# Gated heads: the two widest levels block by block without a mask, the six others masked and summed in the diagonal 32x32 blocks

## The chip, the cores and the metric

The kernel runs on one core of a Trainium2 chip. The metric is device time in microseconds (us) of one execution, as the median of several runs. The engines named below are PE (matrix multiplies), DVE (vector), ACT (activations and copies), POOL and SP (the queue that issues the weight DMAs). Each engine works through its own instructions in order and waits on semaphores for the others.

## The reference, cut to what matters

The whole program is a four-layer model on 256 tokens. The change touches only the gated linear attention in two of the layers: "GLA" with 4 heads (value width 256) and "HGRN" with 8 heads (value width 128).

```
def chunked_gated_linear_attention(q, k, v, log_g):
    '''S_t = diag(g_t) S_{t-1} + k_t^T v_t ; o_t = q_t S_t, evaluated chunkwise.'''
    bc = jnp.cumsum(blocks(log_g), axis=2)
    ...
        inter = jnp.einsum('bihk,bhkv->bihv', qi * jnp.exp(bi), state)
        decay = jnp.exp(jnp.where(causal, bi[:, :, None] - bi[:, None, :], -jnp.inf))
        scores = jnp.einsum('bihk,bjhk,bijhk->bhij', qi, ki, decay)
        intra = jnp.einsum('bhij,bjhv->bihv', scores, vi)
```

## The kernel before

**The stream of weights.** Everything is organised around chunks of 512x512 weights in float32. SP loads chunk i into the ring `WF`. ACT writes its bf16 high half, `hi(i)` (L974), DVE the remainder as a bf16 low half, `lo(i)` (L1464), which waits for `hi(i)`. PE multiplies each chunk in three products per tile, 48 matmuls of 256 columns in `gemm` (L513). ACT and DVE work three chunks ahead (`LA` = 3), on rings of five.

**Flows beside it.** All other work is written as Python generators. Every engine has one queue of such flows (`Side`) and takes a step of the first flow at fixed places: with `rate=3`, ACT and DVE take three steps after each hi or lo, and PE takes one step in the middle of a chunk and two at its end. A flow has the same number of steps on each engine, so step s of a head lies at the same chunk everywhere, but an engine reaches it only after all that is written in front of it. This order is fixed when the program is built.

**A head of the gated attention** (`gla_heads`, once for each engine) works on two halves m of 128 tokens, with the scores split by eight levels: level 0 is the diagonal, level l the pairs that lie in the same block of 2^l tokens but in different halves of it. It takes 8 steps, numbered 0 to 7:

- PE: step 0 products of half 0 (eight 128x128 float32 matmuls into banks 0 and 1 of `PB`, and the cross product into bank 2), step 1 the norm sum of the head in front (it needs bank 2, which the cross copy frees), step 2 products of half 1, step 6 scores times values, `weighted`, which reads `RED`.
- DVE: step 1 and step 3, for half 0 and half 1, multiply the 128x1024 products by the mask `lmask` into `MS` (L1903) and sum over the levels into `RED` (L1907); at step 3 also the scaling of the head in front (L1924, it needs `s_rms`); step 4 `weigh(h+1)`, 16 multiplies (L1893); step 5 `decay(h+2)`, 15 subtractions (L1881 to L1883).
- ACT: step 0 copy and square of the output of the head in front (L1086, L1089), step 1 the cross copy (L1274), step 2 the norm of the head in front by Ln and Exp (L1095, L1097), each with a table load, step 7 the exponentials of h+2 (L1266), which need `decay(h+2)`.

In HGRN, the flow begins late and the heads lie beside the last gate, the `glu` and the `cd_out0` products. Heads are counted from 0 in each layer.

Of the kernel before, what the change touches and what calls it, by code (L numbers as in the profile page):

```python
# [195 lines left out]
def two_block_model(nc, A, out):  # L196
    ctx = ExitStack()
    with ctx:
# [3 lines left out]
        def sem(name):  # L202
# [50 lines left out]
        s_tab, s_tabv, s_cp, s_ang5, s_rot5 = (  # L253
            sem(n) for n in ("s_tab", "s_tabv", "s_cp", "s_ang5", "s_rot5"))

        s_decp, s_gabs, s_lg, s_ones, s_scan, s_dec, s_dexp, s_wgh, s_prod, s_ms, s_cross, s_xc, s_red = (
            sem(n) for n in ("s_decp", "s_gabs", "s_lg", "s_ones", "s_scan", "s_dec", "s_dexp", "s_wgh", "s_prod",
                             "s_ms", "s_cross", "s_xc", "s_red"))
        s_dil, s_gy, s_gh, s_gl = (sem(n) for n in ("s_dil", "s_gy", "s_gh", "s_gl"))

        s_bu, s_br, s_mg, s_sscan, s_xs, s_yb, s_ty, s_uh, s_ul = (
# [173 lines left out]
        def gpsimd_program():  # L435
# [28 lines left out]
            nc.gpsimd.wait_ge(s_xl, x_ready(4)[-1][1])  # L464
            nc.gpsimd.wait_ge(d_csst, 16 * 16)
            nc.gpsimd.wait_ge(d_cwst, 16 * 8)
            t = own.mark(nc.gpsimd.memset(GLA["MS"], 1.0))
            nc.gpsimd.wait_ge(g_own, t)
            nc.gpsimd.memset(GLA["MS"].rearrange("p (m w) -> p m w", w=128)[:, :, 0:1], 0.0).then_inc(s_ones, 1)
# [18 lines left out]
            for n in range(16):  # L488
                if n % 2 == 0 and n // 2 + 2 < 8:
                    nc.gpsimd.wait_ge(s_bu, n + 2)  # L490
                    b_load(n // 2 + 2)
                if n < 14:
                    nc.gpsimd.wait_ge(s_xs, n + 1)
                    rotation_load(n + 2)
                if n % 2 and n < 15:
                    nc.gpsimd.wait_ge(s_yb, n + 1)
                    nc.gpsimd.dma_start(CW, CWD[n // 2 + 1]).then_inc(d_cwld, 16)

        def tensor_program():
# [261 lines left out]
            def gla_heads(P):  # L763
# [3 lines left out]
                def head(h):  # L767
                    n = base + h
                    kk, qq, e = k[:, h, :], q[:, h, :], E[h % 2]
                    for m in range(2):  # L770
                        c = slice(128 * m, 128 * m + 128)
                        nc.tensor.wait_ge(s_wgh, n + 1)
                        free(0)
                        for l in range(8):
                            lhs, rhs = (kk[:, c], qq[:, c]) if l == 0 else (e[:, l - 1, c], e[:, l - 1, c])
                            last = mm(PB[:, l // 4, 128 * (l % 4):128 * (l % 4) + 128], lhs, rhs, l % 4 == 0, True)
                        last.then_inc(s_prod, 1)
                        bank_free[0] = (s_ms, 2 * n + m + 1)
                        if m == 0:
                            free(2)  # L780
                            mm(PB[:, 2, 0:128], e[:, 7, 0:128], e[:, 7, 128:256], True, True).then_inc(s_cross, 1)
                            bank_free[2] = (s_xc, n + 1)
                        yield
                        yield
                    yield
                    yield
                    nc.tensor.wait_ge(s_xc, n + 1)
                    nc.tensor.wait_ge(s_red, 2 * n + 2)
                    weighted(P["v"], 128 * nv * h, nv, RED)
                    yield  # L790
                    yield
# [171 lines left out]
        def scalar_program():  # L963
# [33 lines left out]
            def idle(n):  # L997
                for _ in range(n):
                    yield
# [256 lines left out]
            def gla_heads(P):  # L1256
                H, nv, base, E, RED = P["H"], P["nv"], P["base"], P["E"], P["RED"]

                def exponentials(h):
# [5 lines left out]
                    nc.scalar.wait_ge(s_dec, n + 1)  # L1265
                    act(e, e, ACT.Exp).then_inc(s_dexp, 1)  # L1266

                def head(h):
                    n = base + h
                    yield  # L1270
                    nc.scalar.wait_ge(s_cross, n + 1)
                    if h:
                        nc.scalar.wait_ge(s_pv, P["pv"] + h)
                    act(RED[:, 128:256], PB[:, 2, 0:128], ACT.Copy).then_inc(s_xc, 1)  # L1274
                    yield from idle(6)
                    if h + 2 < H:
                        exponentials(h + 2)
                    yield
# [118 lines left out]
            def hgrn():  # L1397
                while "idd" not in flags:
                    yield
                nc.scalar.wait_ge(s_scan, 2)  # L1400
                nc.scalar.wait_ge(s_ul, 2)
                yield from gla_heads(HGRN)

            nc.scalar.wait_ge(s_gam, 1)
# [49 lines left out]
        def vector_program():  # L1454
# [411 lines left out]


            def gla_heads(P):
                H, nv, base, E, RED, MS = P["H"], P["nv"], P["base"], P["E"], P["RED"], P["MS"]

                def decay(h):
                    n, bb, e = base + h, P["b"][:, h, :], E[h % 2]
# [23 lines left out]
                def head(h):  # L1896
                    n = base + h
                    for m in range(2):
                        yield
                        nc.vector.wait_ge(s_prod, 2 * n + m + 1)  # L1900
                        if 2 * n + m:
                            nc.vector.wait_ge(s_red, 2 * n + m)
                        tt(MS, PB[:, 0:2, :].rearrange("p a b -> p (a b)"), cn("lmask"), ALU.mult).then_inc(s_ms, 1)  # L1903
                        nc.vector.wait_ge(s_ms, 2 * n + m + 1)
                        if h:
                            nc.vector.wait_ge(s_pv, P["pv"] + h)
                        nc.vector.tensor_reduce(RED[:, 256 * m:256 * m + 128], MS.rearrange("p (l t) -> p t l", l=8),  # L1907
                                                AX.X, ALU.add).then_inc(s_red, 1)
                        yield
                    if h + 1 < H:  # L1910
                        weigh(h + 1)
# [336 lines left out]
```

## Time and profile before

| | |
|---|---|
| median of 3 runs | 3239.39 us (3235.76 to 3240.88) |
| the profiled execution: its time, its span | 3238.17 us, 3236.9 us |
| PE busy, share of the span | 3062.1 us, 95% |
| DVE busy | 2151.3 us, 66% |
| ACT busy | 1527.1 us, 47% |
| mean granted clock of PE | 0.978 of full speed |

Matmuls overlap, so PE's busy share says that its queue was seldom empty, not that it was at its peak. What the change can be worth is read from the stretches in which PE waits, and from who is waited for there.

### The profile page before, as it was taken

What the parts mean: (1) busy time and instruction counts of PE and PEld (TensorE: products, weight loads), DVE (VectorE), ACT (ScalarE), POOL (GpSimd) and SP (SyncE); (2) the same over time, 40 slices, a digit from 0 to 9 for tenths busy, and PEclk for the clock granted to TensorE, in tenths of its full rate; (3) what the DMA queues carried; (4) which work ended last, traced back from release to release, by engine and by line L of the source; (5) the groups of instructions that cost most, each with busy time, mean ns of one, the idle gap of its engine ahead of it and who ended that gap; (6) DMA issues with size and microseconds to landing.
All of it is one profiled execution on the core that took longest, in us unless ns stands there. A gap on an engine that the chain in (4) does not pass through costs nothing. (4 is left out here: it accounts for less than half of the span.)

```text
span 3236.9 us, 57237 instructions
## 1 busy us (share of the span) xinstructions
PE 3062.1 (95%) x25845; PEld 2603.8 (80%) x25870; DVE 2151.3 (66%) x2204; ACT 1527.1 (47%) x1406; POOL 64.5 (2%) x112
## 2 busy tenths in 40 slices
PE   8999999999999999999999999998999899888786
PEld 7888788888888787588888888886687777657685
DVE  5555866666555666468687776545765557998785
ACT  4343655444433544745455554335544534324543
POOL 0000000000000000001200000000000001000000
PEclk9999999999999999999999999999999999899898
DMA  8665455565565454455766566553445445554331
GB/s 285 209 208 183 148 204 196 208 209 201 204 206 200 154 180 159 157 169 170 267 228 218 206 224 244 196 182 120 163 149 196 151 163 203 172 189 156 113 118 66
DMA packets 295476, 596.75 MB, mean 184 GB/s; under 512 B 11824, under 2 KB 16048, under 8 KB 295104
## 3 DMA queue, kind: packets, MB, share of 16 engines
q1 hardware_dynamic: 287616, 564.22, 51.1%
q0 software_dynamic: 7616, 28.87, 2.4%
q8 instruction: 203, 3.33, 0.4%
q14 instruction: 41, 0.34, 0.0%
HBM read 577.32 MB, written 15.73 MB: 183 GB/s over the span
## 5 line engine op out<-in xcount | busy, mean ns | idle before, releaser
L1464 DVE TENSOR_TENSOR WL<-WF,WH 128x2048 bf16<-128x2048 f32 x533 | 1206.8, 2285 | 692.6 <-ACT WH L974 692.4
L506 PE MATMUL PSG<-XH,WH 128*128 128x256 bf16 x5648 | 1552.4, 275 | 49.8 <-DVE XL L1569 24.1
L506 PE MATMUL PSG<-XL,WH 128*128 128x256 bf16 x5648 | 1551.7, 275 | 0.0
L506 PE MATMUL PSG<-XH,WL 128*128 128x256 bf16 x5648 | 1551.4, 275 | 0.0
L974 ACT ACTIVATE WH<-WF 128x2048 bf16<-128x2048 f32 x533 | 1000.2, 1899 | 617.2 <-PE PSG L506 381.5
L506 PE MATMUL PSG<-SCR,WH 128*128 128x256 bf16 x4480 | 738.5, 273 | 0.0
L506 PEld LDWEIGHTS PSG<-XH,WH 128*128 128x128 bf16 x5648 | 557.1, 99 | 132.0 <-issue 62.4
L506 PEld LDWEIGHTS PSG<-XL,WH 128*128 128x128 bf16 x5648 | 556.9, 99 | 70.7 <-issue 0.8
L506 PEld LDWEIGHTS PSG<-XH,WL 128*128 128x128 bf16 x5648 | 556.8, 99 | 68.8
L506 PE MATMUL PSG<-SCR,WL 128*128 128x256 bf16 x2240 | 611.2, 273 | 0.0
L506 PEld LDWEIGHTS PSG<-SCR,WH 128*128 128x128 bf16 x4480 | 439.2, 98 | 55.8 <-issue 0.3
L506 PEld LDWEIGHTS PSG<-SCR,WL 128*128 128x128 bf16 x2240 | 219.5, 98 | 25.8
L506 PE MATMUL PB<-SCR 128*128 128x128 f32 (+3 forms) x928 | 165.3, 346 | 56.0 <-DVE SCR L2084 31.0
L506 PEld LDWEIGHTS PB<-SCR 128*128 128x128 f32 (+2 forms) x928 | 137.2, 206 | 78.9 <-DVE SCR L2084 35.6
L1688 DVE SCALAR_TENSOR_TENSOR SCR<-PSG,PR,SCR 128x254 f32<-128x254 f32 (+1 forms) x352 | 143.9, 474 | 52.5 <-ACT SCR L1147 51.4
L1147 ACT ACTIVATE SCR<-PSG,PR 128x256 f32<-128x256 f32 x176 | 85.0, 562 | 100.2 <-PE PSG L506 100.2
L506 PE MATMUL PSG<-WL,XH 128*128 128x512 bf16 x314 | 119.5, 381 | 1.0 <-issue 0.5
L995 ACT ACTIVATE SCR<-PSG 128x1024 f32<-128x1024 f32 x34 | 34.7, 1021 | 181.6 <-PE PSG L506 181.6
L506 PE MATMUL PSG<-WH,XL 128*128 128x512 bf16 x314 | 119.3, 380 | 0.3
L506 PE MATMUL PSG<-WH,XH 128*128 128x512 bf16 x307 | 116.9, 381 | 0.3
L1158 ACT ACTIVATE SCR<-SCR 128x1024 bf16<-128x1024 f32 x22 | 23.3, 1057 | 96.4 <-DVE SCR L1697 96.4
L506 PEld LDWEIGHTS PSG<-WH,XL 128*128 128x128 bf16 x320 | 31.4, 98 | 38.1 <-issue 0.6
(240 smaller groups left out, 1554.2 us busy)
## 6 DMA issues: line engine op xcount, KB each, us to landing
WF<-ffn_w_up SPq DMA_DIRECT2D x176, 1024.0 KB, 5.8
WF<-ffn_w_down SPq DMA_DIRECT2D x88, 1024.0 KB, 5.1
WF<-ab_w_in SPq DMA_DIRECT2D x56, 1024.0 KB, 5.2
WF<-a_w_in SPq DMA_DIRECT2D x48, 1024.0 KB, 5.9
WF<-cd_w_in SPq DMA_DIRECT2D x48, 1024.0 KB, 5.2
WF<-a_w_out SPq DMA_DIRECT2D x16, 1024.0 KB, 5.2
WF<-kv_w_k SPq DMA_DIRECT2D x16, 1024.0 KB, 5.1
WF<-b_w_q SPq DMA_DIRECT2D x16, 1024.0 KB, 5.1
```

The costliest lines, as they stand in the source:

```text
L506: return nc.tensor.matmul(o, lhsT, rhs, start=start, stop=stop, skip_group_check=True)
L974: act(shaped(WH, i % RB, rows, g["width"]), shaped(WF, i % RF, rows, g["width"]), ACT.Copy).then_inc(s_hi, 1)
L995: act(dst, rowwise(ps) if row_major else ps[:, :, :], func, scale=scale).then_inc(s_evac[gi % 2], 1)
L1147: t = act(dst[:, n, :], ps[:, n, :], ACT.Identity, bias=pr("f_bias", 88 * l + f), scale=pr("f_conv", 264 * l + 176 + f))
L1158: act(four(HH, j), HF, ACT.Copy).then_inc(s_hh, 1)
L1464: tt(l, w, h, ALU.subtract).then_inc(s_lo, 1)
L1688: ins = stt(dst[:, n, sh:T], ps[:, n, 0:T - sh], pr("f_conv", 264 * l + 88 * tap + f), dst[:, n, sh:T], ALU.mult, ALU.add)
```

## The change

The products of levels 6 and 7 are no longer computed as full 128x128 matmuls and masked. They are nonzero in one 64x64 block (level 7) and two 32x32 blocks (level 6) only, and PE computes these blocks straight into bank 1. ACT copies them to `RED` (new step `levels`). Levels 0 to 5 lie wholly in the four diagonal 32x32 blocks; DVE masks these with four instructions on 32 partitions x 192 elements, one per block, and sums them with one 128x192 to 128x32 reduction into a corner of `MS`. ACT then copies the four diagonal blocks to `RED` (new step `diagonal`). The rest of `RED` is zeroed once per layer by POOL. `weighted` waits for the new semaphore `s_dg`, the products for `s_lev`.

```diff
# gpsimd_program
+            nc.gpsimd.memset(GLA["RED"], 0.0)
...
+            nc.gpsimd.wait_ge(s_xs, 16)
+            nc.gpsimd.memset(HGRN["RED"], 0.0).then_inc(s_ones, 1)
# tensor_program, gla_heads
-                        free(0)
-                        for l in range(8):
+                        free(0, 1)
+                        for l in range(6):
...
+                        for l, a, w in ((6, 0, 64), (5, 0, 32), (5, 64, 32)):
+                            o, i = 256 + a + w, 128 * m + a
+                            last = mm(PB[a:a + w, 1, o:o + w], e[:, l, i:i + w], e[:, l, i + w:i + 2 * w], False, True)
                         last.then_inc(s_prod, 1)
                         bank_free[0] = (s_ms, 2 * n + m + 1)
+                        bank_free[1] = (s_lev, 2 * n + m + 1)
...
-                    nc.tensor.wait_ge(s_red, 2 * n + 2)
+                    nc.tensor.wait_ge(s_dg, 2 * n + 2)
# scalar_program, gla_heads
+                def levels(n, m):
+                    nc.scalar.wait_ge(s_ms, 2 * n + m + 1)
+                    for a, w in ((0, 64), (0, 32), (64, 32)):
+                        o, i = 256 + a + w, 256 * m + a + w
+                        t = act(RED[a:a + w, i:i + w], PB[a:a + w, 1, o:o + w], ACT.Copy)
+                    t.then_inc(s_lev, 1)
+
+                def diagonal(n, m):
+                    nc.scalar.wait_ge(s_red, 2 * n + m + 1)
+                    for b in range(0, 128, 32):
+                        t = act(RED[b:b + 32, 256 * m + b:256 * m + b + 32], P["MS"][b:b + 32, 192:224], ACT.Copy)
+                    t.then_inc(s_dg, 1)
...
                     act(RED[:, 128:256], PB[:, 2, 0:128], ACT.Copy).then_inc(s_xc, 1)
-                    yield from idle(6)
+                    levels(n, 0)
+                    yield
+                    diagonal(n, 0)
+                    yield
+                    levels(n, 1)
+                    yield
+                    diagonal(n, 1)
+                    yield
+                    yield
+                    yield
# vector_program, gla_heads, for each half m
-                        tt(MS, PB[:, 0:2, :].rearrange("p a b -> p (a b)"), cn("lmask"), ALU.mult).then_inc(s_ms, 1)
...
+                        for b in range(0, 128, 32):
+                            t = tt(some[b:b + 32, :, :], ps[b:b + 32, 0:6, b:b + 32], mask[b:b + 32, 0:6, b:b + 32],
+                                   ALU.mult)
+                        t.then_inc(s_ms, 1)
                         nc.vector.wait_ge(s_ms, 2 * n + m + 1)
-                        if h:
-                            nc.vector.wait_ge(s_pv, P["pv"] + h)
-                        nc.vector.tensor_reduce(RED[:, 256 * m:256 * m + 128], MS.rearrange("p (l t) -> p t l", l=8),
-                                                AX.X, ALU.add).then_inc(s_red, 1)
+                        if 2 * n + m:
+                            nc.vector.wait_ge(s_dg, 2 * n + m)
+                        nc.vector.tensor_reduce(MS[:, 192:224], some.rearrange("p l t -> p t l"), AX.X,
+                                                ALU.add).then_inc(s_red, 1)
```

What stands on ACT at head 3 of HGRN, from the cross copy on. L1274 is the cross copy, L1095 and L1097 the norm of head 2, L974 hi, L1263 and L1266 the exponentials of head 5. Before:

```order
L1274 ACTIVATE SCR<-PB 128x128 [waits s_pv,s_cross]
L1095 ACT_TABLE_LOAD [waits s_nout]
L1095 ACTIVATE STAT<-PB,CN 128x256 [waits s_norm]
L1097 ACT_TABLE_LOAD
L1097 ACTIVATE STAT<-STAT 128x256 [waits s_ln]
L974 ACTIVATE WH<-WF 128x2048 [waits s_mm,d_w2]
L974 ACTIVATE WH<-WF 128x2048 [waits s_mm,d_w0]
L1263 ACTIVATE SCR<-SCR 128x128 [waits s_prod]
L1266 ACTIVATE SCR<-SCR 128x2048 [waits s_dec,a_own]
```

In the change every line number is higher (the cross copy is L1295, the norm L1103 and L1105, hi L982), L1280 is `levels` and L1286 `diagonal`:

```order
L1295 ACTIVATE SCR<-PB 128x128 [waits s_pv,s_cross]
L1280 ACTIVATE SCR<-PB 64x64 [waits s_ms]
L1280 ACTIVATE SCR<-PB 32x32 x2
L1286 ACTIVATE SCR<-SCR 32x32 [waits s_red]
L1286 ACTIVATE SCR<-SCR 32x32 x3
L1103 ACT_TABLE_LOAD [waits s_nout]
L1103 ACTIVATE STAT<-PB,CN 128x256 [waits s_norm]
L1105 ACT_TABLE_LOAD
L1105 ACTIVATE STAT<-STAT 128x256 [waits s_ln]
L982 ACTIVATE WH<-WF 128x2048 [waits s_mm,d_w2]
```

The norm and the next hi now stand behind copies that wait for DVE's mask (`s_ms`) and sum (`s_red`) of this head; before, nothing between the cross copy and that hi waited for DVE's work on this head.

What stands on DVE at the same place, head 3 of HGRN, between the lo of one chunk and the scaling at step 3. L1464 is lo, L1903 the mask, L1907 the sum, L1924 the scaling. Before:

```order
L1464 TENSOR_TENSOR WL<-WF,WH 128x2048 [waits s_hi]
L1903 TENSOR_TENSOR SCR<-PB,CN 128x1024 [waits s_red,s_prod]
L1907 TENSOR_REDUCE SCR<-SCR 128x128 [waits s_pv,s_ms]
L1464 TENSOR_TENSOR WL<-WF,WH 128x2048 [waits s_hi]
L1903 TENSOR_TENSOR SCR<-PB,CN 128x1024 [waits s_red,s_prod]
L1907 TENSOR_REDUCE SCR<-SCR 128x128 [waits s_pv,s_ms]
L1924 SCALAR_TENSOR_TENSOR SCR<-SCR,PR,STAT 128x256 [waits s_rms]
```

In the change lo is L1495, the mask L1938, the sum L1944, the scaling L1961:

```order
L1495 TENSOR_TENSOR WL<-WF,WH 128x2048 [waits s_hi]
L1938 TENSOR_TENSOR SCR<-PB,CN 32x192 [waits s_red,s_prod]
L1938 TENSOR_TENSOR SCR<-PB,CN 32x192 x3
L1944 TENSOR_REDUCE SCR<-SCR 128x32 [waits s_dg,s_ms]
L1495 TENSOR_TENSOR WL<-WF,WH 128x2048 [waits s_hi]
L1938 TENSOR_TENSOR SCR<-PB,CN 32x192 [waits s_red,s_prod]
L1938 TENSOR_TENSOR SCR<-PB,CN 32x192 x3
L1944 TENSOR_REDUCE SCR<-SCR 128x32 [waits s_dg,s_ms]
L1961 SCALAR_TENSOR_TENSOR SCR<-SCR,PR,STAT 128x256 [waits s_rms]
```

The order on DVE is the same: mask and sum of half 0, a lo, mask and sum of half 1. The sum now also waits for ACT's copy of the sum in front (`s_dg`).

## Rows read from the trace of the kernel before

**Rows 1.** Stages: length; busy and count of PE, PEld, DVE, ACT, POOL; PE clock, DMA.

```profile
2350.00:2400.00 50.00, 47.65 (x400) 43.13 (x398) 37.62 (x61) 26.07 (x26) 0.00 (x0) 0.97 0.38 123
3050.00:3100.00 50.00, 36.57 (x297) 32.35 (x295) 36.32 (x70) 27.66 (x29) 0.00 (x0) 0.88 0.30 106
3100.00:3150.00 50.00, 47.08 (x399) 42.54 (x398) 46.99 (x86) 25.60 (x27) 0.00 (x0) 0.95 0.35 118
```

**Rows 2.** Waits, 2990 to 3165 us: total us, times, longest.

```profile
ACT SCR L1266 <- DVE SCR L1883: 40.9, 4, 11.7
PE PB L506 <- ACT SCR L1274: 22.2, 6, 6.2
DVE WL L1464 <- ACT WH L974: 17.2, 9, 4.5
PE PB L506 <- DVE SCR L1903: 6.2, 5, 1.6
```

**Rows 3.** Groups of DVE by form: count, busy us, mean ns, idle before.

```profile
L1907 DVE TENSOR_REDUCE SCR<-SCR 128x128 f32<-128x1024 f32 x24 | 46.2, 1925 | 0.8
L1893 DVE TENSOR_TENSOR SCR<-SCR 128x128 f32<-128x128 f32 x192 | 39.8, 285 | 0.6 <-ACT SCR L1266 0.6
L1903 DVE TENSOR_TENSOR SCR<-PB,CN 128x1024 f32<-128x1024 f32 x24 | 29.2, 1218 | 9.2 <-PE PB L506 9.2
L1743 DVE TENSOR_TENSOR SCR<-SCR 32x1024 f32<-32x1024 f32 x8 | 9.7, 1212 | 0.3
```

**Rows 4.** Groups of ACT by form, the same columns.

```profile
L1387 ACT ACTIVATE SCR<-SCR 128x2 f32<-128x2 f32 x16 | 3.3, 206 | 0.5
L1274 ACT ACTIVATE SCR<-PB 128x128 f32<-128x128 f32 x12 | 3.3, 277 | 4.5 <-PE PB L506 4.5
```

**Rows 5.** Timeline of ACT, head 3 of HGRN: start, length, in us.

```profile
3065.42 1.89 ACT L974 ACTIVATE WH<-WF 128x2048 bf16<-128x2048 f32 x1
...
3067.75 0.28 ACT L1274 ACTIVATE SCR<-PB 128x128 f32<-128x128 f32 x1
3068.04 1.28 ACT L1095 ACT_TABLE_LOAD   x1
...
3071.18 0.42 ACT L1097 ACTIVATE STAT<-STAT 128x256 f32<-128x256 f32 x1
3071.51 3.69 ACT L974 ACTIVATE WH<-WF 128x2048 bf16<-128x2048 f32 x2
```

**Rows 6.** Timeline of DVE, head 3 of HGRN.

```profile
3067.34 2.29 DVE L1464 TENSOR_TENSOR WL<-WF,WH 128x2048 bf16<-128x2048 f32 x1 [3.99 <-ACT WH L974]
3069.55 1.22 DVE L1903 TENSOR_TENSOR SCR<-PB,CN 128x1024 f32<-128x1024 f32 x1
3070.80 1.94 DVE L1907 TENSOR_REDUCE SCR<-SCR 128x128 f32<-128x1024 f32 x1
3073.43 2.29 DVE L1464 TENSOR_TENSOR WL<-WF,WH 128x2048 bf16<-128x2048 f32 x1 [0.69 <-ACT WH L974]
...
3079.13 3.31 DVE L1893 TENSOR_TENSOR SCR<-SCR 128x128 f32<-128x128 f32 x16
```

**Rows 7.** Timeline of PE, head 3 of HGRN.

```profile
3068.17 1.19 PE L506 MATMUL PB<-SCR,ONE 128*128 128x256 f32 x2 [6.19 <-ACT SCR L1274]
3070.91 3.66 PE L506 MATMUL PB<-SCR 128*128 128x128 f32 x16 [1.56 <-DVE SCR L1903]
```

**Rows 8.** Timeline of DVE, head 4 of HGRN: mask of half 0, next lo.

```profile
3097.94 1.22 DVE L1903 TENSOR_TENSOR SCR<-PB,CN 128x1024 f32<-128x1024 f32 x1
...
3102.28 2.29 DVE L1464 TENSOR_TENSOR WL<-WF,WH 128x2048 bf16<-128x2048 f32 x1 [1.16 <-ACT WH L974]
```

**Rows 9.** Timeline of DVE, head 6 of HGRN: mask, next lo, weigh.

```profile
3140.03 1.22 DVE L1903 TENSOR_TENSOR SCR<-PB,CN 128x1024 f32<-128x1024 f32 x1
...
3144.26 2.28 DVE L1464 TENSOR_TENSOR WL<-WF,WH 128x2048 bf16<-128x2048 f32 x1
...
3149.94 3.31 DVE L1893 TENSOR_TENSOR SCR<-SCR 128x128 f32<-128x128 f32 x16
```

More of the change, by code:

```diff
@@ L254, in two_block_model @@
             sem(n) for n in ("s_tab", "s_tabv", "s_cp", "s_ang5", "s_rot5"))
-        s_decp, s_gabs, s_lg, s_ones, s_scan, s_dec, s_dexp, s_wgh, s_prod, s_ms, s_cross, s_xc, s_red = (
+        s_decp, s_gabs, s_lg, s_ones, s_scan, s_dec, s_dexp, s_wgh, s_prod, s_ms, s_cross, s_xc, s_red, s_lev, s_dg = (
             sem(n) for n in ("s_decp", "s_gabs", "s_lg", "s_ones", "s_scan", "s_dec", "s_dexp", "s_wgh", "s_prod",
-                             "s_ms", "s_cross", "s_xc", "s_red"))
+                             "s_ms", "s_cross", "s_xc", "s_red", "s_lev", "s_dg"))
         s_dil, s_gy, s_gh, s_gl = (sem(n) for n in ("s_dil", "s_gy", "s_gh", "s_gl"))
@@ L772, in head @@
                         nc.tensor.wait_ge(s_wgh, n + 1)
-                        free(0)
-                        for l in range(8):
+                        free(0, 1)
+                        for l in range(6):
                             lhs, rhs = (kk[:, c], qq[:, c]) if l == 0 else (e[:, l - 1, c], e[:, l - 1, c])
-                            last = mm(PB[:, l // 4, 128 * (l % 4):128 * (l % 4) + 128], lhs, rhs, l % 4 == 0, True)
+                            mm(PB[:, l // 4, 128 * (l % 4):128 * (l % 4) + 128], lhs, rhs, l % 4 == 0, True)
+                        for l, a, w in ((6, 0, 64), (5, 0, 32), (5, 64, 32)):
+                            o, i = 256 + a + w, 128 * m + a
+                            last = mm(PB[a:a + w, 1, o:o + w], e[:, l, i:i + w], e[:, l, i + w:i + 2 * w], False, True)
                         last.then_inc(s_prod, 1)
                         bank_free[0] = (s_ms, 2 * n + m + 1)
+                        bank_free[1] = (s_lev, 2 * n + m + 1)
                         if m == 0:
@@ L1401, in hgrn @@
                 nc.scalar.wait_ge(s_ul, 2)
+                nc.scalar.wait_ge(s_ones, 4)
                 yield from gla_heads(HGRN)
@@ L1868, in gla_heads @@
             def gla_heads(P):
-                H, nv, base, E, RED, MS = P["H"], P["nv"], P["base"], P["E"], P["RED"], P["MS"]
+                H, nv, base, E, MS = P["H"], P["nv"], P["base"], P["E"], P["MS"]
                 def decay(h):
@@ L1902, in head @@
                             nc.vector.wait_ge(s_red, 2 * n + m)
-                        tt(MS, PB[:, 0:2, :].rearrange("p a b -> p (a b)"), cn("lmask"), ALU.mult).then_inc(s_ms, 1)
+                        ps = PB[:, 0:2, :].rearrange("p a b -> p (a b)").rearrange("p (l t) -> p l t", t=128)
+                        mask = cn("lmask").rearrange("p (l t) -> p l t", t=128)
+                        some = MS[:, 0:192].rearrange("p (l t) -> p l t", t=32)
+                        for b in range(0, 128, 32):
+                            t = tt(some[b:b + 32, :, :], ps[b:b + 32, 0:6, b:b + 32], mask[b:b + 32, 0:6, b:b + 32],
+                                   ALU.mult)
+                        t.then_inc(s_ms, 1)
                         nc.vector.wait_ge(s_ms, 2 * n + m + 1)
-                        if h:
-                            nc.vector.wait_ge(s_pv, P["pv"] + h)
-                        nc.vector.tensor_reduce(RED[:, 256 * m:256 * m + 128], MS.rearrange("p (l t) -> p t l", l=8),
-                                                AX.X, ALU.add).then_inc(s_red, 1)
+                        if 2 * n + m:
+                            nc.vector.wait_ge(s_dg, 2 * n + m)
+                        nc.vector.tensor_reduce(MS[:, 192:224], some.rearrange("p l t -> p t l"), AX.X,
+                                                ALU.add).then_inc(s_red, 1)
                         yield
```

## The prediction

> **What bounds the kernel now.** I read the stages first. In GLA (2350 to 2400) PE is busy 47.65 of 50 us at a granted clock of 0.97, and DVE 37.62; in HGRN (3050 to 3100) PE is down to 36.57 us at 0.88, and in the next 50 us DVE is busy 46.99 us [rows 1]. So the heads matter little to the end in GLA, where the gemm is long enough, and much in HGRN, where they lie beside `cd_out0`.
>
> The waits of 2990 to 3165 say who is late [rows 2]. PE waits 22.2 us for L1274, ACT's cross copy, in 6 waits, and 6.2 us for L1903, DVE's mask. ACT itself waits 40.9 us for L1883, the end of `decay`. DVE waits 17.2 us for hi. The chain is a loop of DVE and ACT: `decay(h+2)` releases the exponentials on ACT, hi stands behind them, the copy of the next head behind hi, lo and mask on DVE behind the same hi, and then DVE's mask, sum, `weigh` and `decay` again.
>
> Head 3 shows it. ACT's hi runs 3065.42 to 3067.31, the cross copy ends at 3068.03, the norm of head 2 follows at once to 3071.60, and then two hi [rows 5]. DVE's lo waits 3.99 us for the first hi, then come mask and sum to 3072.74, a lo at 3073.43 that waited 0.69 us, mask and sum of half 1, `weigh` at 3079.13 [rows 6]. PE waits 6.19 us before the norm sum and 1.56 us for the mask before the products of half 1 [rows 7]. ACT is ahead of DVE after its cross copy: norm and hi are done while DVE masks. That lead is what the change touches.
>
> **The change, part by part.**
>
> *DVE, mask.* A multiply of 128 elements takes 285 ns, of 1024 elements 1218 ns: 1.04 ns an element. 32 partitions cost what 128 do (L1743, 1212 ns) [rows 3]. So one of 192 elements takes 0.35 us. Sixteen multiplies of 128 take 3.31 us [rows 6], so they start 0.20 us apart, 0.08 less than one lasts. With that overlap the four take 3 x 0.27 + 0.35 = 1.16 us, without it 1.41, against 1.22 before. No row shows vector instructions that follow each other on other partitions. I take 1.41 us, the end without overlap, since each starts on other partitions than the one in front. By this the mask alone gains nothing, and each step behind it comes 0.2 us later.
>
> The Trainium skill has a rule for this (VectorE: DVE Perf Modes, section Two Vector instructions with no wait between them): an instruction whose inputs or output start in another group of 32 partitions than those in front is held until all earlier ones have finished. By it the mask takes the 1.41 us; by the overlap of the `weigh` row, 1.16 us, and the sum below would be some 2.5 us less. No row of this trace tests it.
>
> *DVE, sum.* 1925 ns for 1024 elements [rows 3]: in proportion 0.36 us for 192, with some fixed part I take 0.45. A half took 3.19 us (3069.55 to 3072.74) and takes 1.41 + 0.03 + 0.45 = 1.89, so 1.3 us less. Over 24 halves 31 us of DVE work go.
>
> *ACT, new copies.* A copy of 128 elements takes 277 ns, one of 2 elements 206 [rows 4]; each new one is between. Three copies take 0.4 to 0.7 us, four 0.5 to 0.9 us, by how far they overlap. I take 0.5 and 0.6. That is 1.1 x 24 = 26 us of ACT work, on an engine with long idle times. What counts is that they wait for DVE, and what is queued behind them: the norm (3068.04 to 3071.60, 3.5 us), hi (1.9 us), and on DVE the lo that waits for this hi.
>
> *Heads with the chunk's end between step 2 and step 3* (HGRN 2, 3, 4). For head 3, with all up to the mask unchanged: mask 3069.55 to 3070.96, `levels` to 3071.6 (0.1 us for the semaphore), `diagonal` to 3072.2, norm to 3075.7, hi to 3077.5. DVE's lo starts at 3077.5, not 3073.43: 4.1 us later. Behind it half 1 is 1.3 us shorter, so `weigh`, `decay`, the exponentials and the next cross copy come 2.8 us later. Head 2 has the same form, another 2.8. For head 4 the lo started 4.34 us after the mask [rows 8]; now it is 7.95, so 3.6 later, less 1.3: +2.3. Sum of the three: +7.9 us. PE waits on the next cross copy, so it pays in full.
>
> *Heads with the chunk's end between step 1 and 2* (HGRN 1, 6). Only `levels` stands before hi. For head 6: mask 1.41 + 0.1 + 0.5 + hi 1.9 = 3.9 us to the lo, against 4.23 before; then lo 2.2 and half 1 1.9, 8.0 us; the norm (3.9 + 0.6 + 3.5) is done at 8.0 too, the scaling adds 0.4: `weigh` 8.4 us after the mask against 9.91 [rows 9], so 1.5 gained on DVE. At head 6 PE has its own work in front of that `weigh` and brings the delay along, so I count 0; at head 1, 0.5 gained.
>
> *The other heads.* By the same steps: head 0 +1.2 (hi comes behind both masks, and a lo waits for it), head 5 +0.3 (no lo between its halves), head 7 +0.5 (longer mask, two semaphore hops more, before the last `weighted`). HGRN in all: 7.9 - 0.5 + 0 + 1.2 + 0.3 + 0.5 = +9.4 us. GLA: PE is the bound, and what the copies delay is covered by a chunk of gemm; two short waits for the cross copy shrink a little, -0.3. If that cover were gone, its heads would cost like those above.
>
> *PE.* Sixteen instructions of products take 3.66 us after a wait [rows 7], 0.46 us a product, with the clock at its lower level; half at the upper one. Two of eight go, three small ones come, each between nothing and the price of a full one: -0.46 to +0.23 us a half. Where PE is the bound (GLA's 8 halves and a few of HGRN) I take -0.1 each, -1 us; longer waits of PE give more products at the lower level, +1 us. `free(0, 1)` at step 2 makes PE wait for `levels`: +0.7 us after the mask's wait of 1.56, but in the three heads above it is not on the loop.
>
> *POOL.* Two fills of 384 columns, one ahead of the scan, one after S5; both have many us of slack. 0.
>
> **The sum**: +9.4 - 0.3 - 1 + 1 = +9.1 us. The profiled execution took 3238.17 us, 1.2 less than the median of the runs; 3238.2 + 9.1 = 3247.3 on its own scale, and 3248.5 on that of the median. I round to 3248.
>
> **The rivals.**
>
> *DVE's relief wins (faster).* Place: HGRN heads 2 to 6, where DVE is busy 46.99 of 50 us [rows 1]. If lo never waited longer for hi, each of these ten halves would shorten the loop by 1.3 us, 13 us, and PE regains some 2 us at the higher clock: 3224. It decides where the lo after half 0 starts less than 5.2 us after the mask begins (3.9 before plus the 1.3 saved); with norm and hi, 5.4 us by themselves, behind mask and copies it can't, in heads 2 to 4. Against it too: DVE already waits for hi there [rows 2]. 10%.
>
> *The two cancel (no change).* The delay of 4 us meets slack that I don't see: the last of the two hi is early by then, and heads 1 and 6 give back what they gain on DVE (2 x 1.5). Then +1 to +4, about 3241. 20%.
>
> *Small instructions are dear.* All seven copies 0.28 us without overlap (+0.9 a half), sum 0.7 us, PE's small products as dear as full ones: about +1.2 us in each of the eight heads, 3258. 10%.
>
> **How the numbers follow.** Forecast 60%, of which a fifth falls within 0.2% (6.5 us, about what a measurement of this kernel can tell from no change). Slower 0.48 + 0.10 = 0.58; same 0.12 + 0.20 = 0.32; faster 0.10. The forecast's own range is 3243 to 3254 (mask 1.16 or 1.41, copies at either end). Leaving out the faster case and the top of the dear one: 3236 to 3259.
>
> **What would show it.** After: DVE busy some 30 us less, ACT 20 to 30 more. The wait of lo for hi in the HGRN stretch up from 17.2 to near 30 us, with a gap of 5 to 6 us after the sum of half 0 in heads 2 to 4. The norm's table loads behind the small copies. PE's wait for the cross copy up from 22.2 to 27 us or more; GLA's heads within 1 us of before. The mask group near 0.35 us each, and whether four take 1.2 or 1.4. Wrong if those gaps are under 2 us, or if `weigh` of head 4 lies earlier from the mask of head 3 than before.

## The result: slower by 0.6%, twice the size of the sum

| | before | after |
|---|---|---|
| median | 3239.39 us, 5 runs (3233.18 to 3245.92) | 3258.50 us, 5 runs (3256.52 to 3263.54) |
| span of the profiled execution | 3236.9 us | 3256.3 us |
| ratio of the times, 95% interval | | 1.0062 (1.0044 to 1.0080) |

The change costs 19 us, 14 to 26 by the interval of the ratio. The forecast had the direction and the mechanism, and the time lies just inside its range of 3236 to 3259; but the sum was +9.1 us, half of what was measured.

The page of the changed kernel, busy time of each engine:

```profile
PE 3070.6 (94%) x25893; PEld 2603.4 (80%) x25918; DVE 2123.8 (65%) x2276; ACT 1560.9 (48%) x1574; POOL 66.2 (2%) x114
```

DVE is busy 27.5 us less, ACT 33.8 us more, PE 8.5 us more, though two of its eight full products a half have become three small ones. So the change did move work off DVE; the time went up all the same.

Its stages, with the columns of [rows 1]. HGRN's heads now lie some 15 us later, so the second row is taken later too:

```profile
2350.00:2400.00 50.00, 47.07 (x397) 41.49 (x395) 30.94 (x72) 30.52 (x53) 0.00 (x0) 0.97 0.34 108
3065.00:3115.00 50.00, 31.26 (x235) 26.29 (x234) 27.34 (x56) 30.34 (x49) 0.00 (x0) 0.76 0.31 106
3115.00:3165.00 50.00, 44.52 (x378) 38.15 (x376) 41.90 (x108) 31.08 (x60) 0.00 (x0) 0.97 0.38 127
```

In GLA PE is as busy as before and DVE has 7 us less to do. In HGRN PE is busy only 31 us of 50, at a granted clock of 0.76.

Its waits, 2990 to 3185 us:

```profile
DVE WL L1495 <- ACT WH L982: 41.6, 13, 6.3
ACT SCR L1280 <- DVE SCR L1938: 33.0, 12, 4.0
...
PE PB L510 <- ACT SCR L1295: 25.9, 7, 8.2
...
ACT SCR L1274 <- DVE SCR L1914: 18.6, 4, 5.7
PE PB L510 <- ACT SCR L1280: 10.4, 6, 2.9
```

Against [rows 2]: DVE's wait for hi went from 17.2 to 41.6 us. ACT's wait of 40.9 us for `decay` is split: 18.6 are left (in `L1274`, which was `L1266`), and 33.0 are now spent ahead of `levels`, for DVE's mask, with norm and hi queued behind. PE waits 25.9 us for the cross copy (22.2 before) and 10.4 us for `levels`, where it waited 6.2 for the mask.

The new groups, with the columns of [rows 3]:

```profile
L1938 DVE TENSOR_TENSOR SCR<-PB,CN 32x192 f32<-32x192 f32 x96 | 33.9, 353 | 20.9 <-PE PB L510 19.4
L1286 ACT ACTIVATE SCR<-SCR 32x32 f32<-32x32 f32 x96 | 21.7, 226 | 1.3
L1944 DVE TENSOR_REDUCE SCR<-SCR 128x32 f32<-128x192 f32 x24 | 11.6, 482 | 0.8
L1280 ACT ACTIVATE SCR<-PB 32x32 f32<-32x32 f32 x48 | 8.6, 179 | 0.3
L1280 ACT ACTIVATE SCR<-PB 64x64 f32<-64x64 f32 x24 | 5.2, 215 | 51.3 <-DVE SCR L1938 51.3
L510 PE MATMUL PB<-SCR 128*64 128x64 f32 x48 | 8.6, 265 | 0.0
L510 PE MATMUL PB<-SCR 128*32 128x32 f32 x96 | 6.4, 214 | 0.0
```

Head 3 of HGRN after the change, ACT, DVE and PE in three views, to be read against [rows 5 to 7]:

```profile
3074.15 0.28 ACT L1295 ACTIVATE SCR<-PB 128x128 f32<-128x128 f32 x1
3077.56 0.49 ACT L1280 ACTIVATE SCR<-PB 64x64 f32<-64x64 f32 x3 [3.13 <-DVE SCR L1938]
3078.08 0.94 ACT L1286 ACTIVATE SCR<-SCR 32x32 f32<-32x32 f32 x4
3079.04 1.28 ACT L1103 ACT_TABLE_LOAD   x1
...
3082.44 1.89 ACT L982 ACTIVATE WH<-WF 128x2048 bf16<-128x2048 f32 x1
```

```profile
3076.07 1.46 DVE L1938 TENSOR_TENSOR SCR<-PB,CN 32x192 f32<-32x192 f32 x4
3077.56 0.47 DVE L1944 TENSOR_REDUCE SCR<-SCR 128x32 f32<-128x192 f32 x1
3084.37 2.29 DVE L1495 TENSOR_TENSOR WL<-WF,WH 128x2048 bf16<-128x2048 f32 x1 [6.33 <-ACT WH L982]
...
3088.97 3.32 DVE L1924 TENSOR_TENSOR SCR<-SCR 128x128 f32<-128x128 f32 x16
```

```profile
3074.57 1.19 PE L510 MATMUL PB<-SCR,ONE 128*128 128x256 f32 x2 [8.17 <-ACT SCR L1295]
3078.20 3.56 PE L510 MATMUL PB<-SCR 128*128 128x128 f32 x18 [2.43 <-ACT SCR L1280]
```

ACT has finished the cross copy at 3074.43 and stands still for 3.13 us until DVE's mask is done. Then copies, norm and hi follow without a gap, and DVE, which had finished its sum at 3078.03, waits 6.33 us for that hi. Before, this wait was 0.69 us [rows 6]. From the mask to the lo it was 3.88 us, now it is 8.30.

**Where the 19 us arise.** DVE's `weigh` starts once a head, so its starts show what each head adds. The last two rows are ACT's last cross copy and DVE's last evacuation of `cd_out1`. Starts in us from the two traces:

| point | before | after | later by | added | term of the sum |
|---|---|---|---|---|---|
| first cross copy of HGRN | 2988.26 | 2990.08 | 1.8 | 1.8 (GLA and up to here) | -0.3 - 1 |
| `weigh` behind head 0 | 2999.73 | 3003.17 | 3.4 | 1.6 | +1.2 |
| behind head 1 | 3019.97 | 3022.91 | 2.9 | -0.5 | -0.5 |
| behind head 2 | 3047.86 | 3054.27 | 6.4 | 3.5 | +2.8 |
| behind head 3 | 3079.13 | 3088.97 | 9.8 | 3.4 | +2.8 |
| behind head 4 | 3107.97 | 3120.94 | 13.0 | 3.1 | +2.3 |
| behind head 5 | 3131.57 | 3145.03 | 13.5 | 0.5 | +0.3 |
| cross copy of head 7 | 3156.41 | 3171.89 | 15.5 | 2.0 | 0 |
| last evacuation | 3219.19 | 3236.50 | 17.3 | 1.8 | +0.5 + 1 |
| end of the span | 3236.9 | 3256.3 | 19.4 | 2.1 | 0 |

The pattern of the heads is the forecast one, with most terms a little larger; the rest is in front of HGRN and behind head 5, where the sum had nearly nothing.

### The profile page after: what moved, and what is told of

The parts are those of the page before. It is cut to its first block and busy times, and to the rows that moved or that the text cites. A ratio compares the mean times of both kernels' runs of the same rounds, so it can differ in the third digit from the quotient of the medians.

```text
span 3256.3 us, 57578 instructions
## 1 busy us (share of the span) xinstructions
PE 3070.6 (94%) x25893; PEld 2603.4 (80%) x25918; DVE 2123.8 (65%) x2276; ACT 1560.9 (48%) x1574; POOL 66.2 (2%) x114
## 5 line engine op out<-in xcount | busy, mean ns | idle before, releaser
L1495 DVE TENSOR_TENSOR WL<-WF,WH 128x2048 bf16<-128x2048 f32 x533 | 1206.8, 2285 | 716.7 <-ACT WH L982 716.5
L982 ACT ACTIVATE WH<-WF 128x2048 bf16<-128x2048 f32 x533 | 1000.4, 1899 | 612.1 <-PE PSG L510 379.0
L510 PE MATMUL PB<-SCR 128*128 128x256 f32 (+5 forms) x976 | 168.3, 337 | 63.2 <-DVE SCR L2121 31.8
L510 PEld LDWEIGHTS PB<-SCR 128*128 128x128 f32 (+4 forms) x976 | 135.2, 194 | 93.0 <-DVE SCR L2121 36.6
```

Source lines behind the costliest of these rows:

```text
L510: return nc.tensor.matmul(o, lhsT, rhs, start=start, stop=stop, skip_group_check=True)
L982: act(shaped(WH, i % RB, rows, g["width"]), shaped(WF, i % RF, rows, g["width"]), ACT.Copy).then_inc(s_hi, 1)
L1495: tt(l, w, h, ALU.subtract).then_inc(s_lo, 1)
```

## The experiments

Each was timed in 5 rounds beside the kernel before; a ratio is to the kernel before, with its 95% interval. The kernels of the first heading ran together, and so did those of the second, so their times compare directly. Under the third, full_products, before_ahead_all and after_ahead_all ran later than the rest, on another chip. The change itself was timed in none of these groups; against it, and between groups, the ratios are compared.

### Is it the copies' work, or where they wait?

Theory A: the copies cost by standing in front of norm and hi while they wait for DVE. Rival B: their work on ACT costs, wherever it stands.

**before_copies**: the kernel before, plus seven copies a half at the places of `levels` and `diagonal`.

```diff
+                def extra(k, wait_for, pieces):
+                    if wait_for is not None:
+                        nc.scalar.wait_ge(*wait_for)
...
+                    for a, w, c in pieces:
+                        t = act(SPARE[a:a + w, c:c + w], CN[a:a + w, 0:w], ACT.Copy)
```

> The kernel before, with seven small ACT copies a half (64x64, 32x32, 32x32 at one step, four 32x32 at the next) between constants and a spare tile, at the steps where the change has its copies, but waiting for nothing of DVE; PE and DVE are as before. Theory A (the copies cost because they wait for DVE, with the norm and hi queued behind them): the work alone, 34 us on an engine with long idle times, costs 0 to 3 us, so 3239 to 3242 us, and DVE's waits for hi in the HGRN stretch stay near 17 us. Theory B (ACT's added work itself fills the loop): 1.4 us a half in heads 1 to 6, so +12 to +17 us, near 3254 us.

**before_waits**: the same, with `wait_for` set to DVE's mask and sum of the half.

```diff
-                        extra(2 * k, None, ((0, 64, 0), (0, 32, 64), (64, 32, 0)))
+                        extra(2 * k, (s_ms, 2 * n + m + 1), ((0, 64, 0), (0, 32, 64), (64, 32, 0)))
```

> As before_copies, but the three copies wait for DVE's mask and the four for DVE's sum of the same half, as in the change; PE and DVE are as before, so DVE saves nothing. Theory A: in HGRN heads 2, 3, 4 the lo after half 0 comes 1.2 + 1.9 + 0.1 + 0.9 + 3.5 + 1.9 = 9.6 us after the mask starts, instead of 3.9 to 4.3, so 5.5 us more a head, with 2 to 4 us in the other heads: +18 to +21 us, near 3259 us, with three gaps of some 6 us before those lo. Theory B: no more than before_copies.

Measured: before_copies 3247.23 us, 1.0022 (1.0013 to 1.0031), between the two expectations; before_waits 3267.98, 1.0088 (1.0074 to 1.0101). Before stood at 3240.24. The waits of before_waits, 2990 to 3185 us:

```profile
DVE WL L1486 <- ACT WH L976: 38.6, 12, 6.3
PE PB L507 <- ACT SCR L1289: 33.0, 7, 11.1
```

In before_copies DVE waits 25.6 us for hi, 4.5 at most. So the work costs 7 us and the waits 21 more, and the gap of 6.3 us comes with the waits. Both add to 28 us; the change costs 19, so what else it does gives some 9 us back, above all the mask and sum of 1.96 us a half on DVE instead of 3.19. ACT was not as idle as I took it to be: before_copies runs its seven copies end to end between cross copy and norm, with nothing waited for.

```profile
3072.38 0.28 ACT L1289 ACTIVATE SCR<-PB 128x128 f32<-128x128 f32 x1
3072.54 1.56 ACT L1280 ACTIVATE SPARE<-CN 64x64 f32<-64x64 f32 x7
3074.12 1.28 ACT L1097 ACT_TABLE_LOAD   x1
```

**norm_first**: the change, with ACT's norm of the head in front moved ahead of `levels`.

```diff
...
                     act(RED[:, 128:256], PB[:, 2, 0:128], ACT.Copy).then_inc(s_xc, 1)
+                    next(last, None)
                     levels(n, 0)
...
```

> The change, with one edit: ACT takes the norm of the head in front (Ln, Exp and their table loads) at step 1, right behind the cross copy and ahead of levels, instead of at step 2 behind diagonal. The work is the same. Theory A: in heads 2, 3, 4 the norm again runs while DVE masks, hi comes 2.5 to 3.5 us earlier and the lo with it, 8 to 10 us in all, so 3248 to 3251 us; levels come up to 1 us later, which PE waits for before the products of half 1. Theory B: the same 3258 us as the change, within 2 us.

Measured: 3258.18 us, 1.0059 (1.0046 to 1.0072), no gain. Its lo waits, from DVE's timeline:

```profile
3021.81 2.29 DVE L1500 TENSOR_TENSOR WL<-WF,WH 128x2048 bf16<-128x2048 f32 x1 [7.99 <-ACT WH L982]
...
3083.03 2.29 DVE L1500 TENSOR_TENSOR WL<-WF,WH 128x2048 bf16<-128x2048 f32 x1 [3.26 <-ACT WH L982]
```

The gaps of heads 2 to 4 fell from 6.33 to 3.27, 3.26 and 3.74 us, as expected, but head 1's grew from 4.45 to 7.99 and head 6's from 0.72 to 3.37: there the norm used to stand behind hi and now stands in front. The expectation counted the heads that gain and not those that lose. A reorder at step level can't serve both, since the end of a chunk falls at another step in each head.

**hi_ahead**: the change, with ACT four chunks ahead instead of three from the end of S5 to `cd_out1`.

```diff
+            look = [LA]
-                    hi_to(g["first"] + c + LA)
+                    hi_to(g["first"] + c + look[0])
...
             side.until(s5_flow)
+            look[0] = LA + 1
```

> The change, with one edit: from the end of the S5 flow to the start of cd_out1, ACT writes hi four chunks ahead instead of three, so that each hi stands one chunk earlier in its queue; DVE stays three ahead. Theory A: DVE never waits long for hi in heads 2 to 4, the three gaps of 6.33 us close to under 1 us, and 12 to 16 us come back: 3243 to 3247 us (less if hi then waits for PE to leave its slot of the ring). Theory B: the same 3258 us as the change, within 2 us.

Measured: 3230.62 us, 0.9973 (0.9962 to 0.9984), 28 us under the change and 12 below the expectation. ACT and then DVE at head 3:

```profile
3069.76 0.28 ACT L1296 ACTIVATE SCR<-PB 128x128 f32<-128x128 f32 x1
3069.91 0.47 ACT L1281 ACTIVATE SCR<-PB 64x64 f32<-64x64 f32 x3
3070.41 0.94 ACT L1287 ACTIVATE SCR<-SCR 32x32 f32<-32x32 f32 x4
```

```profile
3067.59 1.46 DVE L1941 TENSOR_TENSOR SCR<-PB,CN 32x192 f32<-32x192 f32 x4
3069.08 0.48 DVE L1947 TENSOR_REDUCE SCR<-SCR 128x32 f32<-128x192 f32 x1
3069.48 2.28 DVE L1498 TENSOR_TENSOR WL<-WF,WH 128x2048 bf16<-128x2048 f32 x1
```

With hi in hand, the lo follows the sum at once in heads 2 to 4, and at head 3 DVE is no longer late for `levels` either. Heads 0 and 1 still wait 1.97 and 4.46 us for hi. That the copies' waits cost through the late hi is shown: where hi comes earlier, the cost is gone, as the comparison with before_hi_ahead below confirms.

### Which layer, and is the gain of hi_ahead the change's?

**gla_only** and **hgrn_only** make the change in one layer's heads alone, by a condition at each part of it. This is PE's in gla_only; hgrn_only has `base > 0`.

```diff
-                        for l in range(6):
+                        new = base == 0
+                        for l in range(6 if new else 8):
```

> The change in the four GLA heads alone; HGRN is computed as in the kernel before. Theory A (the prediction's miss lies partly in GLA, where PE has no slack to hide late products, dearer small matmuls and the stretches at the lower clock that follow its waits): 2 to 4 us above the kernel before, 3242 to 3244, with the last GLA norm sum some 2.5 us later. Rival B (the prediction: GLA's heads are covered by a chunk of gemm): 0 to 1 us below the kernel before, 3238 to 3240, all of the rise in HGRN.

> The change in the eight HGRN heads alone; GLA is computed as before. Theory A: 15 to 17 us above the kernel before, 3255 to 3257, so that this and gla_only add up to the change. Rival B (all of it in HGRN): 19 us, 3258 to 3260. The prediction's own size for HGRN was 9.4 us, 3249.

Measured: gla_only 3239.72 us, 1.0003 (0.9994 to 1.0012); hgrn_only 3255.24, 1.0052 (1.0039 to 1.0066); before 3238.70. The last cross copy in each (before 3156.41, after 3171.89), first gla_only, then hgrn_only:

```profile
3158.02 0.28 ACT L1297 ACTIVATE SCR<-PB 128x128 f32<-128x128 f32 x1 [1.35 <-PE PB L507]
```

```profile
3170.68 0.28 ACT L1299 ACTIVATE SCR<-PB 128x128 f32<-128x128 f32 x1 [1.54 <-PE PB L509]
```

+1.6 and +14.3 add to 15.9 against the change's 15.5, so the two layers' costs add up. HGRN costs some 16.5 us where I had 9.4; of the 14.3, 0.7 us is already there at HGRN's first cross copy (2988.99 against 2988.26), in front of every changed head, so single traces are good to about that. In GLA the traces show 1.6 to 1.8 us, which the times can't tell from nothing: 3239.72 lies in rival B's range, and theory A's 2 to 4 us is at the upper end of the interval.

**before_hi_ahead**: the kernel before with the edit of hi_ahead.

> The kernel before with the same look-ahead of four chunks for ACT's hi in the last layer's stretch, and none of the change. Theory A (the change has a gain of its own, DVE's 31 us less work, that only the late hi hid): this saves no more than 3 us, since DVE's mask and sum then set the loop, 3237 to 3240, and the change with hi ahead stays 7 to 10 us faster. Rival B (the look-ahead does it all, it takes away DVE's waits for hi of before too, 17 us in 9 waits): 3225 to 3231, level with the change or below it.

Measured: 3227.09 us, 0.9970 (0.9959 to 0.9981); hi_ahead stood at 0.9973. So rival B holds: with hi one chunk earlier in the last layer, the kernel takes the same time with or without the change. The look-ahead takes 28 us off the change and only 12 off the kernel before; the 16 between them are most of what the change cost. A gain of the change's own doesn't show here. Between 2990 and 3185 us DVE still waits 9.4 us for hi in hi_ahead, 2.9 here, and 14.2 us for PE's products there, 5.0 here: in the change the products of half 1 wait for `levels`, which waits for the mask of half 0.

**one_mask**: one mask of 128x192 in place of four of 32x192.

```diff
-                        for b in range(0, 128, 32):
-                            t = tt(some[b:b + 32, :, :], ps[b:b + 32, 0:6, b:b + 32], mask[b:b + 32, 0:6, b:b + 32],
-                                   ALU.mult)
+                        t = tt(some, ps[:, 0:6, 0:32], mask[:, 0:6, 0:32], ALU.mult)
```

> The change with one mask instruction of 128 partitions x 192 elements in place of the four of 32 x 192; it reads the first 32 columns of each level for all partitions, so three of the four diagonal blocks are left out of the scores. DVE's mask falls from 1.45 us to about 0.36. Theory A (mask, sum and copies lie one behind the other on the loop of DVE and ACT in HGRN): both halves of heads 1 to 6 come 1.1 us earlier, 10 to 13 us in all, 3245 to 3248. Rival B (norm and hi behind them set the loop whatever the mask takes, since ACT's work is the bound): 0 to 3 us, 3255 to 3258.

Measured: 3239.83 us, 1.0009 (1.0001 to 1.0018), 17 us under the change by the ratios. Its group:

```profile
L1937 DVE TENSOR_TENSOR SCR<-PB,CN 128x192 f32<-128x192 f32 x24 | 8.5, 353 | 23.1 <-PE PB L510 23.0
```

353 ns, as long as one of the four. So 1.1 us less a half, 24 times 1.1 = 26 us of DVE work, and 17 of them reach the end, more than either expectation. Already HGRN's first cross copy lies at 2981.4 us, 8.6 before the change's, so the split of the mask costs in GLA too. PE's clock was higher there too: it was granted in full between 2360 and 2380 and from 2450 to 2550 us, where the change has 0.91 and 0.98. How much of the 8.6 us the clock alone makes stays open.

### The other split, and PE's side

**one_diagonal**: one copy of 128x32 in place of the four of 32x32.

> The change with one ACT copy of 128x32 in place of the four of 32x32 in the step diagonal; the diagonal blocks of RED then hold other values, so the scores are wrong in three of four blocks. The step falls from 0.94 us to about 0.25. Theory A (everything from mask to hi lies one behind the other in heads 2 to 4 and half of it in heads 0, 5 and 7): 0.7 us in each of four to six heads of HGRN, 3 to 5 us, 3253 to 3256. Rival B (as one_mask, more than the loop alone: each microsecond taken off either half of every head counts): 24 times 0.7, 12 to 17 us, 3242 to 3247.

Measured: 3251.58 us, 1.0046 (1.0033 to 1.0060), 5 us under the change by the ratios, before at 3240.53. That is the upper end of theory A's 3 to 5 us and far from rival B's 12 to 17; but the interval overlaps the change's, so that it is a gain at all is likely and not certain. One copy of 128x32 takes 225 ns, as one of 32x32 does (226), so the split costs 0.7 us a half, and of these 17 us about a third reaches the end.

**blocks** keeps the result and removes the mask's split. PE computes levels 0 to 5 as 24 products of 32x32, which land in columns 0 to 191 of bank m, so one 128x192 mask does for all; the mask tile is gathered once per layer.

```diff
-                        for l in range(6):
...
+                        for l in range(6):
+                            f, g = (kk, qq) if l == 0 else (e[:, l - 1, :], e[:, l - 1, :])
+                            for b in range(0, 128, 32):
+                                i = slice(128 * m + b, 128 * m + b + 32)
+                                mm(PB[b:b + 32, m, 32 * l:32 * l + 32], f[:, i], g[:, i], l == 0, True)
...
+                        t = tt(MS[:, 0:192], PB[:, m, 0:192], MS[:, 256:448], ALU.mult)
```

> The change, but PE computes levels 0 to 5 as 24 products of 32x32 instead of six of 128x128, into columns 0 to 191 of bank m for half m, so that DVE masks all four blocks with one instruction of 128x192 (with a mask gathered once per layer) and the products of half 1 do not wait for the mask of half 0. Theory A (small products cost 67 ns each, as the group of 96 in the change: 1.6 us against 1.5 for six full ones, and the split of the mask was the price): as one_mask or better, 3232 to 3241. Rival B (24 small products on PE cost about 0.2 us each, 3 us more a half, on an engine that is the bound in GLA): 3250 to 3275.

**blocks_hi_ahead** adds the edit of hi_ahead, and **blocks_ahead_all** sets the four chunks from the start of GLA's heads on.

> blocks with ACT's hi four chunks ahead in the last layer's stretch. Theory A (with the mask's split and the late hi both gone, DVE's relief of some 2.3 us a half shows): 10 to 18 us under before_hi_ahead's 3227, 3209 to 3217. Rival B (PE's own work and its clock are then the bound in HGRN, and the relief stays off the path): 3220 to 3228.

> blocks_hi_ahead with the four chunks of look-ahead from the start of the GLA heads on. Theory A (in GLA too DVE waits for hi, 30 us in 11 waits between 2290 and 2410 in the change, and PE waits behind it): 3 to 8 us less than blocks_hi_ahead. Rival B (PE is the bound there, these waits are off the path): within 2 us of it.

Measured: blocks 3238.92 us, 1.0000 (0.9991 to 1.0008); blocks_hi_ahead 3211.97, 0.9921 (0.9907 to 0.9934); blocks_ahead_all 3187.44, 0.9843 (0.9829 to 0.9858). All go the way of theory A. The last is 24.5 us under blocks_hi_ahead where 3 to 8 were expected; what makes the rest stays open. PE and DVE of blocks at head 3:

```profile
3066.35 1.19 PE L510 MATMUL PB<-SCR,ONE 128*128 128x256 f32 x2 [10.10 <-ACT SCR L1296]
3067.47 1.53 PE L510 MATMUL PB<-SCR 128*32 128x32 f32 x54
```

```profile
3067.73 0.35 DVE L1938 TENSOR_TENSOR SCR<-PB,SCR 128x192 f32<-128x192 f32 x1
3068.11 0.48 DVE L1943 TENSOR_REDUCE SCR<-SCR 128x32 f32<-128x192 f32 x1
3074.92 2.29 DVE L1496 TENSOR_TENSOR WL<-WF,WH 128x2048 bf16<-128x2048 f32 x1 [6.33 <-ACT WH L983]
```

The 27 small products of a half take 1.53 us where the change's nine take 3.56, mask and sum take 0.86 us instead of 1.96, and PE no longer waits for `levels` there. The gap of 6.33 us in front of the lo is untouched, and PE's wait grows to 10.10 us: freed time goes into the wait for hi until hi comes earlier.

**full_products**: the change, with PE computing all eight levels in full and ACT copying the blocks out of them.

```diff
-                        for l in range(6):
+                        for l in range(8):
...
-                    for a, w in ((0, 64), (0, 32), (64, 32)):
-                        o, i = 256 + a + w, 256 * m + a + w
+                    for l, a, w in ((7, 0, 64), (6, 0, 32), (6, 64, 32)):
+                        o, i = 128 * (l % 4) + a + w, 256 * m + a + w
```

> The change with PE's products as before: all eight levels as full 128x128 products, ACT copying the blocks of levels 6 and 7 out of them; mask, sum, copies and waits are those of the change. Theory A (six full and three small products take what eight full ones took: 2.37 us against 2.17 for half 0 and 1.95 both for half 1): within 3 us of the change, 3256 to 3260. Rival B (the prediction's term: 0.1 us saved in each of the halves where PE is the bound, up to 0.46 in all): 3 to 8 us slower than the change, 3261 to 3266.

**before_ahead_all** and **after_ahead_all** give the kernel before and the change the wide look-ahead.

> The kernel before with ACT's hi four chunks ahead from the start of the GLA heads to the end. Theory A (the late hi costs in GLA as well as in HGRN, whatever the heads do): before_hi_ahead's 3227 less the 20 to 25 us that the wider look-ahead brought beside blocks_hi_ahead, 3202 to 3207. Rival B (DVE's mask and sum of 3.2 us a half are then the bound, so it gives less here than with DVE relieved): 3212 to 3224.

> The change with the same wider look-ahead. Theory A (the change has no value of its own: its seven copies and four masks a half take from the loop what the shorter sum gives): within 4 us of before_ahead_all. Rival B (its relief of DVE shows once hi is never late): 8 to 15 us faster than before_ahead_all. In either case slower than blocks_ahead_all's 3187 by about 15 us, the price of the split mask.

Measured, before at 3236.99: full_products 3260.96 us, 1.0066 (1.0052 to 1.0080), the change's ratio within both intervals; before_ahead_all 3215.45, 0.9935 (0.9922 to 0.9947); after_ahead_all 3207.95, 0.9910 (0.9897 to 0.9924). DVE's waits for hi between 2960 and 3160 us are all but gone, first in before_ahead_all, then in after_ahead_all:

```profile
DVE WL L1467 <- ACT WH L975: 0.8, 1, 0.8
```

```profile
DVE WL L1498 <- ACT WH L983: 0.7, 1, 0.7
```

In GLA, between 2290 and 2410 us, 10.1 and 11.1 us of them are left. With hi on time in HGRN, the kernel before is still at 3215, in rival B's range, and the change is 7.5 us faster than it, just under rival B's 8 to 15. The intervals of the two ratios overlap by a hair, so the sign is likely and the size rough. blocks_ahead_all is clearly ahead of both, 21 to 22 us under after_ahead_all by the ratios where 15 were expected.

## Why the prediction was right in kind and half in size

**What held.** The copies that wait for DVE push norm and hi back, and lo waits: the gap after the sum of half 0 is 6.33 us in heads 2 to 4, where I wrote 5 to 6, and before_waits makes it in the kernel before with the copies alone. Head 1 gives back 0.5 us to the digit, and head 5 costs 0.5 where 0.3 stood. The mask takes 1.45 us (1.41 taken) and the sum 0.48 (0.45). Of the other signs, DVE's relief (27.5 us) came as stated; ACT's added work (33.8 us) and DVE's wait for hi (41.6 us) went well over their 20 to 30 and near 30, PE's wait for the cross copy stayed just under its 27 (25.9), and GLA ended 1.8 us later where I allowed 1. The Trainium skill's rule (VectorE: DVE Perf Modes, section Two Vector instructions with no wait between them), that an instruction which starts in another group of 32 partitions waits for all in front, agrees with this: four instructions of 353 ns take 1.45 us, none overlapping.

**The step that failed is the sizing of the sum's terms.** Their kind was right, but +9.1 us stood where 19.4 were measured between the two traces. Three groups of terms hold the missing 10.3 us:

- *Behind head 5*, 1.5 taken, 5.9 measured: the largest miss. For heads 6 and 7, "PE has its own work in front", I counted 0 and 0.5, and for all of PE's lower clock 1 us. What the traces show: the products of half 0 take 0.2 us more in each head, and the wait for `levels` at head 7 is 0.62 instead of 0.36 for the mask. At head 6, PE's norm sum and the gemm behind it, up to the products of half 1, take 4.71 us instead of 3.12, the same 26 instructions at a granted clock of 0.66 instead of 1.00 (the two rows below, before and after). PE had waited 2.3 us there; before the change it waited 2.9 us at the same place and kept the full clock, so the wait's length alone doesn't decide it. The last stretch, from the last evacuation to the end, with the same instructions, took 19.8 us against 17.7, with a granted clock of 0.58 against 0.75, and in other kernels of this study lasts 17.7 to 20.0 us. How much of these 1.6 and 2.1 us belongs to the change stays open.
- *GLA and the terms of PE in front of HGRN*, -1.3 taken, +1.8 measured. "What the copies delay is covered by a chunk of gemm" holds nearly: gla_only is at 1.0003. The -1 us for fewer products was wrong: half 0 takes 2.37 us (2.17 before), half 1 1.95 both times, and full_products, which undoes the edit on PE, is no slower than the change.
- *Heads 2 to 4*, 7.9 us taken, 10.0 measured. `diagonal` was put at 0.6 us and takes 0.94, because its four copies don't overlap; that moves the lo of each head: 4.4 us later in head 3 instead of 4.1. Half 1 gives back 1.1 us instead of 1.3. Together 0.5 us a head, 1.5 of the 2.1; head 0, with both terms in it, has 0.4 more.

```profile
3140.78:3143.90 3.12, 3.12 (x26) 2.72 (x27) 3.09 (x3) 3.09 (x3) 0.00 (x0) 1.00 0.73 259
3154.37:3159.08 4.71, 4.71 (x26) 3.58 (x27) 3.91 (x5) 4.02 (x9) 0.00 (x0) 0.66 0.66 223
```

One reading was too kind: "norm and hi are done while DVE masks". The norm was done while DVE summed, but the first of the two hi ended at 3073.4, 0.6 us after DVE's sum [rows 5, 6], and the lo already waited 0.69 us for it. ACT's lead was used up before the change.

**The rivals.** "DVE's relief wins" was priced at 13 us, with the condition that lo never waits longer for hi. Hi on time is needed, but it isn't enough for 13 us: with the look-ahead in the last layer alone the change gains nothing on the kernel before, and with the wide one 7.5 us. "The two cancel" fails, there was no slack. "Small instructions are dear" came out nearest in time, 3258, by luck as much as by reason: the four copies of `diagonal` don't overlap and PE's small products save nothing, both as it said, but the seven copies take 1.43 us a half and not 1.96, the sum of 0.7 us did not come, and the costs fall in three heads and at the ends rather than evenly on eight.

## What to carry to other kernels

A chain of small steps that waits for a slower engine is paid for by what is queued behind it: seven copies a half cost 7 us of work here, and 21 more for standing in front of norm and hi while they wait. Before work is taken off an engine, see whether that engine waits for something late: as long as hi came late, DVE's freed time turned into a longer wait, while one more chunk of look-ahead on ACT brought the kernel before 12 us over the last stretch and 22 us from GLA on. Cutting a tile into partition groups multiplies instructions and not speed on DVE and ACT; let PE put the blocks side by side, so that one instruction of 128 partitions covers them (blocks, 20 us under the change).

## What the hardware showed that was not expected

- *PE, small products in four partition groups.* In blocks the 27 products of a half, 26 of them 32x32 and one 64x64, go to four groups of output partitions in turn. They take 1.07 us at the full clock and 1.53 after a wait; eight full ones took 1.95, and six full with three small ones take as long as eight. The Trainium skill (TensorE: Matmul & The Clock Gate, Part 3: Packing small matmuls) says that products which go to different groups of 32 output partitions run concurrently; its measured gain for these is with 512 columns. The trace agrees: 0.04 us a product, where a quarter of a full product's 0.24 us, for a quarter of its columns, would be 0.06. No run sends the same products to one group, so the gain by the groups alone isn't measured.
- *ACT, copies in turn on four groups of partitions.* Four copies of 32x32 of 226 ns, each on another group, take 0.94 us: no overlap. The three copies of `levels`, the first two of which start on the same partition, take 0.49 us where their lengths add to 0.573 (0.215 + 2 x 0.179), and three with the same pattern in before_copies 0.59 us for 0.691. The Trainium skill (ScalarE: Activation LUTs, section What ACT_TABLE_LOAD costs) gives 93 ns of overlap between activations in a row; two hi in a row agree with it (3.69 us for twice 1.89 [rows 5]), four copies on four groups don't, and the measurement decides. All of this fits an overlap of some 0.09 us between two ACT instructions that start on the same partitions, and none where the group changes; no run was made to test that.
